# Split-precision products in a fused transformer and MoE kernel: from three 256-column passes to one of 256 and one of 512

## What is computed

```
for l in range(2):
    h = rms_norm(x, norm_g[l, 0])
    x = x + 0.5 * (silu(h @ w_gate) * (h @ w_up)) @ w_down      # 1024 -> 2816 -> 1024
    h = rms_norm(x, norm_g[l, 1])
    qa, ka, va, qd, kd, vd, qc, kc, vc = split(h @ w_in[l])      # 1024 -> 3840
    ya = neighbourhood_attention(qa, ka, va, na_rpb[l])          # 8 heads
    yb = diff_attention(qd, kd, vd, lam, ...)                    # 4 heads, 2 softmaxes each
    yc = window_gqa(qc, kc, vc, sink, ...)                       # 8 heads
    g = sigmoid(h @ w_gate[l] + b_gate[l])                       # 1024 -> 3 x 1024
    merged = g0 * (ya @ w_branch0) + g1 * (yb @ w_branch1) + g2 * (yc @ w_branch2)
    x = x + merged @ w_o[l]
    h = rms_norm(x, norm_g[l, 2])
    x = x + 0.5 * swiglu(h, second feed-forward of the layer)
x = rms_norm(x)
```

## Time and profile before

| what | value |
|---|---|
| median of the runs (lowest to highest) | 2224.42 us (2220.97 to 2229.49) |
| the profiled execution | 2220.84 us |
| span of its trace | 2218.9 us |
| TensorE matmuls busy | 2090.0 us, 94% |
| TensorE weight loads busy | 1694.3 us, 76% |
| VectorE busy | 1187.9 us, 54% |
| ScalarE busy | 632.8 us, 29% |
| mean granted TensorE clock | 0.979 |
| bytes read from memory | 467.96 MB |

### The profile page before, as it was taken

How to read it: one execution, slowest core, us unless ns; L and a number is a source line. 1 busy time by engine, 2 the same in 40 slices (tenths; PEclk the granted TensorE clock), 3 DMA queues, 4 the chain that set the end, 5 groups by cost and what they waited for, 6 DMA issues and landing times.

```text
span 2218.9 us, 33949 instructions
## 1 busy us (share of the span) xinstructions
PE 2090.0 (94%) x14045; PEld 1694.3 (76%) x14045; DVE 1187.9 (54%) x2050; ACT 632.8 (29%) x934; POOL 0.2 (0%) x4
## 2 busy tenths in 40 slices
PE   7999999999999999999999999979893999999997
PEld 7999998779999999999878999968573444334443
DVE  6665658774655655666885555553556222222212
ACT  4433434423333533344441433320321000000000
POOL 0000000000000000000000000000000000000000
PEclk9999999999999999999999999989996999999999
DMA  7966552238866666654233676512321899999994
GB/s 227 281 204 181 169 166 84 86 114 225 263 211 195 196 212 204 181 171 152 67 114 106 229 234 210 164 39 76 133 103 69 333 416 416 415 416 415 416 417 186
DMA packets 287144, 471.36 MB, mean 212 GB/s; under 512 B 17306, under 2 KB 223188, under 8 KB 286988
## 3 DMA queue, kind: packets, MB, share of 16 engines
q1 hardware_dynamic: 285680, 466.19, 61.3%
q10 hardware_dynamic: 1308, 2.96, 0.5%
HBM read 467.96 MB, written 1.13 MB: 211 GB/s over the span
## 4 chain that ended last, share of the span: by engine, by line
PE 82%; DMA 10%; DVE 5%; ACT 1%; issue 1%; SPq 1%; DVEq 0%; ACTq 0%
PE ps L618 81%; DMA ring_zone<-in_moe_w_up_dram 5%; DMA ring_over<-in_moe_w_gate_dram 4%; DMA W<-in_ffn_w_gate_dram 1%; PE ps L903 1%; DVE QK L1838 1%; SPq L556 0%; PE ps L1038 0%; DVE hl L1564 0%; DVE hT L1616 0%; DVE WL L1553 0%; DVE xT L1571 0%; DMA PT<-in_norm_g_dram 0%; PE ps L1156 0%; ACT WH L1243 0%
## 5 line engine op out<-in xcount | busy, mean ns | idle before, releaser
L1553 DVE TENSOR_TENSOR WL<-W,WH 128x1024 fp32r<-128x1024 f32 x372 | 453.0, 1223 | 341.9 <-ACT WH L1243 341.9
L618 PE MATMUL ps<-hh,WH 128*128 128x256 f32 x2128 | 610.1, 287 | 12.2 <-DVE WL L1553 6.6
L618 PE MATMUL ps<-hh,WL 128*128 128x256 f32 x2128 | 601.5, 283 | 0.0
L618 PE MATMUL ps<-hl,WH 128*128 128x256 f32 x2128 | 601.4, 283 | 0.0
L1243 ACT ACTIVATE WH<-W 128x1024 fp32r<-128x1024 f32 x372 | 391.5, 1056 | 496.8 <-PE ps L618 472.6
L618 PEld LDWEIGHTS ps<-hh,WH 128*128 128x128 f32 x2128 | 403.0, 189 | 33.0 <-issue 30.1
L618 PEld LDWEIGHTS ps<-hl,WH 128*128 128x128 f32 x2128 | 402.8, 189 | 0.2
L618 PEld LDWEIGHTS ps<-hh,WL 128*128 128x128 f32 x2128 | 402.8, 189 | 0.0
L618 PE MATMUL ps<-ring_over,XT 128*64 128x512 f32 x896 | 204.7, 596 | 24.4 <-DMA ring_over<-in_moe_w_up_dram 13.3
L618 PE MATMUL ps<-hid_h,WH 128*128 128x256 f32 x704 | 202.9, 288 | 0.0
L618 PE MATMUL ps<-hid_h,WL 128*128 128x256 f32 x704 | 198.7, 282 | 0.0
(11 more groups left out here) (315 smaller groups left out, 2338.4 us busy)
## 6 DMA issues: line engine op xcount, KB each, us to landing
ring_over<-in_moe_w_gate_dram SPq DMA_DIRECT2D x128, 512.0 KB, 14.8
ring_zone<-in_moe_w_down_dram SPq DMA_DIRECT2D x128, 512.0 KB, 15.1
ring_over<-in_moe_w_up_dram SPq DMA_DIRECT2D x96, 512.0 KB, 15.4
W<-in_ffn_w_gate_dram SPq DMA_DIRECT2D x88, 512.0 KB, 5.0
W<-in_ffn_w_up_dram SPq DMA_DIRECT2D x88, 512.0 KB, 4.0
W<-in_ffn_w_down_dram SPq DMA_DIRECT2D x88, 512.0 KB, 3.7
W<-in_w_in_dram SPq DMA_DIRECT2D x78, 512.0 KB, 3.9
W<-in_w_gate_dram SPq DMA_DIRECT2D x48, 512.0 KB, 3.6
```

The lines of the kernel that those rows point to most:

```text
L618: ins = nc.tensor.matmul(o, lhsT, rhs, start=start, stop=stop, skip_group_check=True, **kw)
L1553: v.tensor_tensor(low, W[:, i % RAW, :], high.bitcast(F32), ALU.subtract).then_inc(low_ready, 1)
```

## The change

`beside` replaces `mm3` in the gate, up, projection and attention-gate products. It first moves the 256 high columns past the low part of the stationary operand, then the 256 high and the 256 low columns together, as one pass of 512, past the high part. The result is therefore two halves of a bank that have to be added. To make the 512 columns one operand, `WH` and `WL` become one tile `WHL`, `hh` and `hl` become `hhl`, and `hid_h`, `hid_l` become `hid_hl`. The down products keep `mm3`.

Each 256-column result now fills a whole bank: gate and up take two working banks each, as does every projection tile, and the attention gates use banks 0 to 3. `two_banks` reserves both before the first matmul. VectorE adds the halves with `joined`, a `tensor_reduce` over pairs of columns 256 apart (128 x 256 out of 128 x 512 in), and scales afterwards from SBUF. Silu waits for the new semaphore `gated`, the attention loop for `proj_ready`.

```diff
+            def beside(bank, stat, mov, start, stop, then=None, at=0):
+
+                n = mov.shape[2]
+                mm(bank[:, at:at + n], stat[:, 1], mov[:, 0], start, False)
+                mm(bank[:, at:at + 2 * n].rearrange("p (a n) -> p a n", a=2), stat[:, 0], mov, False, stop, then=then)
...
+            def two_banks():
+
+                banks = [begin()]
+                turns.step()
+                banks.append(begin())
+                turns.step()
+                return banks
...
-                            mm3(bank[:, f * T:(f + 1) * T], at(w, j * 256 + f * P), h_at(k),
-                                half + f + j == 0, k == KD - 1, then=then if f and k == KD - 1 else None)
+                            beside(banks[f], at(w, j * 256 + f * P), h_at(k), k == 0, k == KD - 1,
+                                   then=work_ready if k == KD - 1 else None)
...
-                                mm3(ps[:, m % 2, f * T:(f + 1) * T], at(w, j * 256 + f * P),
-                                    h_at(4 * (i % 2) + j), i % 2 + f + j == 0, last,
-                                    then=gate_done if f and last else None)
+                                beside(ps[:, 2 * (m % 2) + f, :], at(w, j * 256 + f * P), h_at(4 * (i % 2) + j),
+                                       i % 2 + j == 0, last, then=gate_done if f and last else None)
...
+            def joined(dst):
+
+                bank = take()
+                give(v.tensor_reduce(dst, bank.rearrange("p (a t) -> p t a", a=2), AX.X, ALU.add))
...
             def ffn(l, i):
                 for b in range(FF_BLOCKS):
                     used(2)
                     if b == 0:
                         used(2)
+                    for f in range(2):
+                        joined(sg[:, b % 2, f * T:(f + 1) * T])
+                    given()
+                    if b == 0:
                         norm_factor()
-                    bank = take()
-                    give(v.tensor_tensor(by_two(sg[:, b % 2, :]), by_two(bank), factor_by_two(), ALU.mult))
+                    scale_by_factor(sg[:, b % 2, :]).then_inc(gated, 1)
                     if b:
                         used(2)
-                    bank = take()
-                    give(v.tensor_tensor(by_two(hid_f[:, b % 2, :]), by_two(bank), factor_by_two(), ALU.mult))
+                    for f in range(2):
+                        joined(hid_f[:, b % 2, f * T:(f + 1) * T])
                     given()
+                    link(scale_by_factor(hid_f[:, b % 2, :]))
...
-                            v.tensor_tensor(gT[:, (branch % 2) * 8 + i - 1:(branch % 2) * 8 + i + 1, :],
-                                            by_two(ps[:, (l * 12 + s // 2) % 2, :]), factor_by_two(), ALU.mult)\
-                                .then_inc(gate_scaled, 1)
+                            g2 = gT[:, (branch % 2) * 8 + i - 1:(branch % 2) * 8 + i + 1, :]
+                            at = 2 * ((l * 12 + s // 2) % 2)
+                            link(v.tensor_reduce(g2, ps[:, at:at + 2, :].rearrange("p f (a t) -> p f t a", a=2), AX.X, ALU.add))
+                            v.tensor_tensor(g2, g2, factor_by_two(), ALU.mult).then_inc(gate_scaled, 1)
```

More of the change, by code:

```diff
@@ L289, in build @@
         moe_const = sb("moe_const", [P, 2 * P])
-        hl = sb("hl", [P, KD, T], FR)
         def zone(*wanted):
@@ L393, in build @@
         h_ready = ev("normed_ready")
+        gated = ev("gate_rows_scaled")
         sg_ready = ev("silu_ready")
@@ L399, in build @@
         p_ready = ev("probs_ready")
+        proj_ready = ev("projection_ready")
         gate_ready = ev("tanh_ready")
@@ L741, in norm, with two_tiles @@
                 turns.step()
-            def two_tiles(kind, bank, h_wait=False, then=None):
+            def two_banks():
[4 more added lines that the diff above has]
+                return banks
+            def two_tiles(kind, h_wait=False):
+                banks = two_banks()
                 for half in range(2):
@@ L832, in _ @@
                                 if c == 14:
-                                    mm3(bank[:, 0:T], at(w, j * 256), h_at(k), k == 0, end)
-                                n, v0 = (P, T) if c == 14 else (256, 0)
+                                    beside(banks[0], at(w, j * 256), h_at(k), k == 0, end,
+                                           then=work_ready if end else None)
                                 for tt in range(TT):
-                                    mm3(bank[:, v0 + tt * n:v0 + (tt + 1) * n], h_at(k, tt * P, P),
-                                        at(w, j * 256 + 256 - n, n), k == 0 and tt == 0 and c != 14, end,
-                                        then=work_ready if end and tt else None)
+                                    if c == 14:
+                                        beside(banks[1], h_at(k, tt * P, P), at(w, j * 256 + P), k == 0 and tt == 0,
+                                               end, then=work_ready if end and tt else None, at=tt * T)
+                                    else:
+                                        beside(banks[tt], h_at(k, tt * P, P), at(w, j * 256, 256), k == 0, end,
+                                               then=work_ready if end else None)
                             done_pair()
-                    proj[c] = turns.step()
                     if c == 0:
@@ L1769, in _ @@
                         link(v.tensor_copy(rstd_of[:, :], ps[:, 0, 0:TT]))
-                    if c in (4, 5, 10, 11):
-                        at = (c - 4) * 256 if c < 6 else 512 + (c - 10) * 256
+                    two = S[:, c % 2, :]
+                    if c == 14:
+                        joined(two[:, 0:T])
+                        given()
+                        v.tensor_tensor(QK[:, 20, :], two[:, 0:T], rstd[:, :], ALU.mult)
+                        v.tensor_tensor(QK[0:64, 21, :], two[64:128, 0:T], rstd[0:64, :], ALU.mult)
+                        v.tensor_tensor(QK[64:128, 21, :], two[0:64, 0:T], rstd[64:128, :], ALU.mult)
+                        bank = take()
+                        give(v.tensor_reduce(by_two(two[:, T:2 * T]),
+                                             bank.rearrange("p (t a n) -> p t n a", t=TT, a=2), AX.X, ALU.add))
+                        given()
@@ new lines, in _ @@
+                    else:
+                        for f in range(2):
+                            joined(two[:, f * T:(f + 1) * T])
+                        given()
+                        if c in (4, 5, 10, 11):
+                            at = (c - 4) * 256 if c < 6 else 512 + (c - 10) * 256
+                            for tt in range(TT):
+                                ins = v.tensor_scalar(V[:, tt, at:at + 256], two[:, tt * 256:(tt + 1) * 256],
+                                                      rstd_of[:, tt:tt + 1], None, ALU.mult)
+                        else:
+                            tile = {0: 0, 1: 2, 2: 4, 3: 6, 6: 8, 7: 10, 8: 12, 9: 14, 12: 16, 13: 18}[c]
+                            scale = HD ** -0.5 if c in (0, 1, 6, 7, 12, 13) else 1.0
+                            ins = v.scalar_tensor_tensor(out=QK[:, tile:tile + 2, :], in0=by_two(two), scalar=scale,
+                                                         in1=factor_by_two(), op0=ALU.mult, op1=ALU.mult)
@@ L1789, in _ @@
+                    link(ins)
+                    v.tensor_copy(rt[:, 0, 0:1], eps[:, :]).then_inc(proj_ready, 1)
                 for s in range(36):
```

71 lines of the change are left out of this document (30 added, 41 removed).

## The result

The changed kernel takes 2242.8 us (2241.6 to 2244.3, 4 runs) where the kernel before takes 2225.2 in the same session: a ratio of 1.0085, 95% interval 1.0068 to 1.0102. It is 0.85% slower. I had forecast 2200, with 2226 as the upper end: the sign is wrong and the range missed it by 17 us.

What follows compares the result with a forecast made beforehand. TensorE's own pace was taken as the bound, VectorE's in early attention steps; -46.7 us from TensorE and +23.1 from waits gave 2197.2 against the profiled execution, 2200.8 on the median's scale; forecast 2200, range 2178 to 2226.

Steps and rivals of the forecast that it cites:

- TensorE's term: All changed products: wide ones 334.5 instead of 355.5 ns, a gain of 21 ns each; together -46.7 us.
- each pass keeps its own 11.8 ns: Bound and rival for the wide products: long pass 225 ns, gain only 12 ns, 2219 us in all; chance 0.15.
- The 32 narrow products: Projection products of 128 columns: 336 ns become 112 + 118.5, a gain of 105 ns each, -3.4 us.
- signs of error: Long pass 225 ns or more before its successor, a join over 1 us, or TensorE waiting for `WHL` within feed-forward blocks.
- The dear join: Rival on VectorE: a join takes 1.33 us and the gate form 2.5; +36 us, 2236 in all; chance 0.13.
- Projection tile 2: TensorE waits 5.4 us for tile 0's banks, read out only after the norm factor; both layers, +10.8 us.
- +1.7 for both places: Lower clock after the waits at projection tile 2, about 0.9 us lost in each layer.
- Attention: Steps 0 to 11: VectorE becomes the bound, a pair of steps 11.4 us, 0.4 longer; +4.8 us for two layers.
- The entry into the loop: Last projection tile leaves VectorE 1.4 us more before step 0, half of it felt; +1.4 us for two layers.
- the later steps: Attention from step 12: VectorE keeps room, so that half of the gate products gains 4.0 us.
- Feed-forward: Block 1 waits +2.4 us, second stages lose +2.0 to loads; VectorE otherwise covered, 13.1 of 16.8 us a block.
- block 1: Feed-forward, first stage of each layer: joins behind a subtraction make TensorE wait 1.2 us; +2.4 us.

Runs made afterwards that it cites:

- joins first: Changed kernel with the two joins of the first projection tile moved ahead of the norm factor: 2225.3 us, ratio 1.0007.
- both repairs: Changed kernel with the first projection tile's joins ahead of the norm factor and the gate products as before the change: 2215.6 us, ratio 0.9962.

## Why the prediction was wrong

**TensorE's term: 34 of the 47 us by which the sum missed the difference of the spans.** "I take 216 for the new pass and leave the short one at 118.5, since the next load still has to fit behind it: 334.5 ns, a gain of 21 ns." This step failed. It rested on the full float32 records and on the reading that the 11.8 ns over streaming are an exposed load. Passes alone show 13.5 ns at 256, 384 and 512 columns, and no less with 32 columns of weights; the 112 ns of the narrow passes say nothing of the wider ones. The bound that I had written down, "each pass keeps its own 11.8 ns", was the truth about the long pass, and even it was generous: in turns the short pass rises from 118.5 to 120.5 ns and the long one stands at 230.5, so that of its 12 ns 4.6 remain. 16.4 ns too many on the 1408 + 464 + 192 products that I had counted are 34 us. The 32 narrow products, counted at 105 ns, did gain that. In the last projection tile one wide product and two narrow ones follow one another eight times; the starts of the first and the eighth group, before and after:
```profile
314.94 0.22 PE L618 MATMUL ps<-WH,hh 128*128 128x128 f32 x1
...
322.13 0.22 PE L618 MATMUL ps<-WH,hh 128*128 128x128 f32 x1
```
```profile
325.36 0.62 PE L619 MATMUL ps<-WHL,hhl 128*128 128x128 f32 x4
...
331.01 0.62 PE L619 MATMUL ps<-WHL,hhl 128*128 128x128 f32 x4
```
7.19/7 = 1.027 us a group became 5.65/7 = 0.807; less the 4.6 ns of the wide product, each narrow one gained 108 ns.

I put the row of another data type above the rows of this one, in a case where only two distances of float32r (128 and 256 columns) were in the trace. The same 11.8 ns had two readings, and the sum took one at its best value.

Two of the signs of error that I had named came true: the long pass starts 225 ns or more before its successor, and TensorE waits for `WHL` within feed-forward blocks.

**The dear join**, the rival that I had for the slower side, is refuted: 683 and 1220 ns. Its 2236 us, the nearest to the measured time, would have been luck. The kernel became slower without it, since the gain that should have paid for the waits was not there.

**Projection tile 2: the wait right, its price undersized.** 5.06 us against 5.4. For the clock I wrote "+1.7 for both places"; it was 2.5 us at the first and 2.8 at the second. In layer 0, 5.06 + 2.5 us, less 232 x 4.6 ns (1.1) and 16 narrow products (1.7), make +4.8, and +5.1 in layer 1; the stage grew by 4.9 and 5.1. The value for the clock came from a place where TensorE was busy 4.3 of 8 us; here it had stood nearly still for 5. The repair with the joins first shows that the place is worth 12.7 us in two layers.

**Attention: the bound right, the account incomplete.** "VectorE becomes the bound and a pair of steps 0.4 us longer" was 0.59 in the first pairs. That VectorE sets the pace there shows in the kernel with the long pass split: its first four gate banks span 34.92 us, as in the changed kernel (34.93), though its products are 5 ns longer; with the gates as before they span 32.62. The entry into the loop was 0.53 us later in each layer, where I had 0.7. By step 11 each layer is 3.7 us late, entry included, against my 3.1, but 1.5 us of that comes back by step 17, where a pair takes 11.73 us instead of 12.97. The gain of 4.0 us that I had for the later steps was nearly absent: the two pairs behind that one are 0.12 us shorter each.

What I had not seen is the end of the loop. In step 23 the last gate reduction stands ahead of the last head's normalisation, which TensorE waits for. The wait, before and after:
```profile
479.17 0.66 PE L903 MATMUL ps<-C,S 128*128 128x128 f32 x4 [0.44 <-DVE S L1865]
```
```profile
494.03 0.66 PE L921 MATMUL ps<-C,S 128*128 128x128 f32 x4 [1.70 <-DVE S L1907]
```
1.26 us in each layer; with the gates as before it is 0.43 again.

A further 2.5 us of the first layer and 1.0 of the second lie in one pair of steps of the last branch (16.65 and 16.82 us between two gate reductions, 14.10 and 15.86 before), behind a wait. The windows there, the kernel after:
```profile
440.00:456.00 16.00, 10.51 (x47) 7.02 (x46) 12.63 (x17) 7.41 (x12) 0.00 (x0) 0.95 0.06 19
456.00:466.00 10.00, 10.00 (x31) 7.03 (x32) 9.61 (x20) 4.15 (x13) 0.00 (x0) 0.57 0.47 157
```
and the kernel before at the same place of its program:
```profile
445.00:455.00 10.00, 10.00 (x53) 7.16 (x52) 9.57 (x22) 5.55 (x16) 0.00 (x0) 0.87 0.47 157
```
The clock after this wait was 0.57 for ten microseconds, 0.87 before the change, though both kernels wait there; the wait only grew from 3.67 to 3.70 us. In the kernel with both repairs it was 1.00. Over the nine traces this pair of steps takes from 12.9 us, at full clock, to 16.8; in the kernel with the joins first, whose loop is that of the changed kernel, it is 15.8 in both layers. So the 2.5 us are not to be put down to the change. Why the clock falls so differently was not settled.

**Feed-forward: waits that I had covered.** Of the block's bursts I wrote "a freed weight pair is needed only three pieces, 8 us, later". TensorE's timeline of the kernel after:
```profile
31.95 4.43 PE L619 MATMUL ps<-hhl,WHL 128*128 128x256 f32 x24 [0.60 <-DVE S L1727]
```
```profile
54.31 3.90 PE L619 MATMUL ps<-hhl,WHL 128*128 128x256 f32 x21 [1.08 <-DVE WHL L1571]
```
```profile
121.92 1.67 PE L619 MATMUL ps<-R,C 128*128 128x384 f32 x4 [1.95 <-DVE S L1727]
```
The first is block 1, forecast at 1.2 us. The second is the wait for `WHL` that I had named as a sign of error, the third a bias table that wants a bank while two tiles still wait for their joins, which stand behind a subtraction of VectorE that ends at 121.27. That subtraction was late because of the loads, since ScalarE, which rounds the weights for it, had itself waited for them:
```profile
118.95 1.06 ACT L1261 ACTIVATE WHL<-W 128x1024 fp32r<-128x1024 f32 x1 [2.42 <-DMA W<-in_ffn_w_gate_dram]
```
The same wait of TensorE was 0.63 us with the joins first, 4.34 with the gates as before, where ScalarE waited 1.8 and 2.9 us for transfers, and 1.57 with the feed-forward as before the change; with both repairs it is absent. The late transfers differ from trace to trace, and this is much of why the first stage does.

Eight such waits of joins and low weights in the four stages, 0.59 to 1.95 us each, 7.9 in all (1.1 before), and a clock of 0.96 around the third one, take what 1408 x 4.6 ns = 6.5 us give and 2.5 more. The forecast had +4.4 for all of them.

**The rest held:** the bytes, the small copies for `proj_ready` and the wait for `gated` cost nothing that shows.

## What to carry to other kernels

Before wider passes are counted as a gain, measure the pace of this data type at both widths: dropping a pass saves at most its fixed part, here 4 to 5 ns a product of 13.5, and the 0.69 us that an added join costs VectorE for eight products must be compared with 37 ns, not with the 168 that I had. Where a change halves the tiles that a ring of banks holds, look for each place where the consumer does something long first (a norm factor), and put the reads that free banks ahead of it: the same 5 us wait also cost 2.5 us of lower clock. A change that bundles four places can hold gains and losses; taken apart, two small edits made it 0.4% faster than the kernel before.

## What was not expected of the hardware

- A float32r pass costs 13.5 ns beside its columns from 256 columns on (120, 173, 227 ns), a bf16 pass 2.5 ns (109, 216), and a load of 32 columns of weights instead of 128 does not lower it (118 and 232 ns).
- Short and long passes in turn cost more than their sum: 351 ns in the kernel and 353 alone, against 347.
- The granted clock after a wait of some 5 us was 0.66 over the next 7 us, and 0.57, 0.87 and 1.00 over some ten at one and the same place of three kernels.
- A reduction that adds two halves of a bank 256 elements apart costs what a `tensor_tensor` of that input does: 683 ns for 512 elements (691), 1220 for 1024 (1223).
